# Four full-width RMS norms of a three-block transformer kernel taken apart and folded into the blocks around them

## What is computed

```python
def rmsnorm(x, g):
    xf = x.astype(jnp.float32)
    xf = xf * lax.rsqrt(jnp.mean(xf * xf, axis=-1, keepdims=True) + EPS)
    return xf.astype(x.dtype) * g
...
        u_lat = rmsnorm(h_lat, norms[layer]) * (1 + scale_l[:, None]) + shift_l[:, None]
        u_ctx = rmsnorm(h_ctx, norms[layer]) * (1 + scale_c) + shift_c
...
        hm = _rmsnorm(x, g_mlp)
        x = x + jnp.square(jax.nn.relu(hm @ w_mlp_in)) @ w_mlp_out

    return _rmsnorm(x, g_final)
```

## Time and profile before

| | |
|---|---|
| median of 3 runs | 4933.83 us |
| lowest, highest | 4932.54, 4934.83 us |
| the profiled execution | 4934.28 us |
| span of its profile | 4932.6 us |
| mean granted clock of TensorE | 0.957 |

### The profile page before, as it was taken

How to read it: one execution, slowest core, us unless ns; L and a number is a source line. 1 busy time by engine, 2 the same in 40 slices (tenths; PEclk the granted TensorE clock), 3 DMA queues, 4 the chain that set the end, 5 groups by cost and what they waited for, 6 DMA issues and landing times. The chain is left out here.

```text
span 4932.6 us, 48010 instructions
## 1 busy us (share of the span) xinstructions
PE 4491.0 (91%) x18750; PEld 2645.4 (54%) x18750; DVE 1475.2 (30%) x3439; ACT 941.5 (19%) x1645; POOL 108.7 (2%) x189
## 2 busy tenths in 40 slices
PE   4999998999979999688396999999999979999997
PEld 2676666775537695377142457466454434444443
DVE  2226663662121454344314421111323110000001
ACT  2223332331034111133202421111111010000000
POOL 0000000000000000011001000001000000000000
PEclk8999999999989999799697999999999989999998
DMA  4220003111000111342102110112223111111111
GB/s 182 88 73 8 8 7 71 47 52 69 16 33 29 57 49 52 69 80 43 61 26 73 33 36 30 57 52 77 88 79 115 34 34 39 39 39 39 39 39 43
DMA packets 150801, 258.91 MB, mean 52 GB/s; under 512 B 68545, under 2 KB 91922, under 8 KB 148775
## 3 DMA queue, kind: packets, MB, share of 16 engines
q1 hardware_dynamic: 142664, 240.77, 15.5%
q0 software_dynamic: 7936, 15.35, 1.2%
HBM read 214.82 MB, written 43.53 MB: 52 GB/s over the span
## 5 line engine op out<-in xcount | busy, mean ns | idle before, releaser
L407 PE MATMUL mlp_prod<-sbuf 128*128 128x512 f32 x2048 | 881.2, 593 | 21.3 <-DMA sbuf<-in_w_mlp_in 21.3
L2494 PE MATMUL lat_banks<-sbuf 128*128 128x512 f32 (+2 forms) x2368 | 847.8, 517 | 22.1 <-DMA sbuf<-in_w_in 22.1
L407 PEld LDWEIGHTS mlp_prod<-sbuf 128*128 128x128 f32 x2048 | 389.8, 190 | 512.7 <-issue 490.6
L2494 PEld LDWEIGHTS lat_banks<-sbuf 128*128 128x128 f32 x2368 | 429.1, 206 | 401.3 <-issue 376.9
L1968 PE MATMUL gla_prod<-sbuf 128*128 128x512 f32 (+1 forms) x784 | 324.1, 570 | 27.8 <-DMA sbuf<-in_l_w_in 27.8
L1485 PE MATMUL mls_banks<-sbuf 128*128 128x512 f32 (+1 forms) x768 | 283.9, 524 | 6.8 <-DMA sbuf<-in_l_w_in 6.3
L1968 PEld LDWEIGHTS gla_prod<-sbuf 128*128 128x128 f32 x784 | 149.1, 194 | 183.6 <-issue 150.7
L1485 PEld LDWEIGHTS mls_banks<-sbuf 128*128 128x128 f32 x768 | 144.1, 192 | 123.4 <-issue 109.1
L224 ACT ACTIVATE sbuf<-sbuf 128x1024 f32<-128x1024 f32 (+2 forms) x56 | 56.7, 1024 | 749.6 <-PEq L67 557.1
L2704 ACT ACTIVATE sbuf<-lat_banks 128x512 f32<-128x512 f32 (+1 forms) x124 | 72.3, 583 | 662.0 <-PE lat_banks L2494 610.6
L1030 PE MATMUL mla_banks<-sbuf 128*128 128x512 f32 (+1 forms) x416 | 176.0, 511 | 0.0
(11 more groups left out here) (373 smaller groups left out, 5446.5 us busy)
## 6 DMA issues: line engine op xcount, KB each, us to landing
sbuf<-in_l_w_in SPq DMA_DIRECT2D x59, 512.0 KB, 3.7
sbuf<-in_w_in SPq DMA_DIRECT2D x52, 512.0 KB, 3.7
sbuf<-in_w_mlp_in SPq DMA_DIRECT2D x32, 512.0 KB, 3.5
sbuf<-in_w_mlp_out SPq DMA_DIRECT2D x32, 512.0 KB, 3.4
sbuf<-in_l_w_mod SPq DMA_DIRECT2D x12, 1024.0 KB, 10.2
sbuf<-in_l_w_mod SPq DMA_DIRECT2D x24, 512.0 KB, 4.8
scratch_gates<-sbuf SPq DMA_DIRECT2D x48, 256.0 KB, 2.9
sbuf<-scratch_gates SPq DMA_DIRECT2D x8, 1536.0 KB, 6.7
```

The lines of the kernel that those rows point to most:

```text
L407: last = nc.tensor.matmul(prod[:, n % NB, o:o + 512], w[:, n % NB, k * P:(k + 1) * P], rhs, start=k == 0, stop=k == KD - 1)
L2494: last = nc.tensor.matmul(dst, lhsT, rhs, start=k == 0, stop=k == KD - 1)
```

## The change

Four of the norms ("norm0", "norm1", "mlpnorm", "final2") stop being stages. Each is cut into three parts.

**Sums.** In the block ahead, ACT squares each slab as soon as it is final, and DVE (in `modulation`: POOL) adds the squares up in one tile `total`. Then eight or ten matmuls with one moving column (`column_sums`, L107) turn the tile of sums into `rcol`, one column per 128 tokens.

**Root.** ACT's root and DVE's reciprocal work on those ten (eight, four) columns alone.

**Scaling.** At the head of the next block PE spreads the columns over 128 partitions again, as broadcast weights against the identity (`spread`, L114), DVE scales H into U, and ACT adds the shift, by thirds of the tokens (512, 512, 256; in the MLP by halves). PE's first tile waits for each slab of each third (`normed`). In `mla_block` three memsets of DVE stand ahead of the scaling, and ACT's and DVE's other work of that block behind it.

The load of H moves from the first stage into `modulation`, as eight DMAs on ACT's queue beside the weights on SP's. The g of layer 1 is loaded in `mlstm_block`, g of the MLP and of the last norm in `mlp_block`. In `mlp_block` the last eight down steps become 16 steps of 8 matmuls, first all slabs of one half of the tokens, then all of the other, with their weights held in U; the last norm of the first half runs behind the products of the second, and each finished piece of 128 by 512 is written out by a DMA of its own. Semaphores cleared at the two clearing points are 112 and 128 where they were 100 and 137.

```diff
+def column_sums(nc, bank, acc, ones, tiles):
+    for t in tiles:
+        last = nc.tensor.matmul(bank[:, t:t + 1], acc[:, t * P:(t + 1) * P], ones[:, 0:1], start=True, stop=True)
+    return last
+def spread(nc, bank, rcol, ident, tiles):
+    for a, t in enumerate(tiles):
+        last = nc.tensor.matmul(bank[:, a * P:(a + 1) * P], rcol[:, t:t + 1].broadcast_to([P, P]), ident[:], start=True, stop=True)
+    return last
...
 # modulation
+            for k in range(KD):
+                act.dma_start(H[:, k, :], io["h"][:, k * T:(k + 1) * T]).then_inc(h_in[k], 16)
...
+            for k in range(KD):
+                act.wait_ge(h_in[k], 16)
+                if k >= 3:
+                    act.wait_ge(added, k - 2)
+                nc.scalar.activation(sq[:, k % 2, :] if k else total[:], H[:, k, :], ACT.Square).then_inc(hsq, 1)
+            act.wait_ge(ssum, 1)
+            nc.scalar.activation(rcol[:, 0:TT], stat[:, 0:TT], ACT.Sqrt, bias=eps, scale=1.0 / D).then_inc(rooted, 1)
+        def _(pool):
+            for k in range(1, KD):
+                pool.wait_ge(hsq, k + 1)
+                pool.drain()
+                nc.gpsimd.tensor_tensor(total[:], total[:], sq[:, k % 2, :], ALU.add).then_inc(added, 1)
...
 # mla_block, and with mod1 and GL gla_layer
+                        if t == 0:
+                            pe.wait_ge(normed, KD * (n - first_of[0]) + kk + 1)
...
+            def shift(c):
+                o, wd = thirds()[c]
+                for k in range(KD):
+                    act.wait_ge(lifted, KD * c + k + 1)
+                    for a, n, v in halves_of(o, wd):
+                        last = nc.scalar.activation(U[:, k, a:a + n], U[:, k, a:a + n], ACT.Identity, bias=mod[:, k, v:v + 1])
+                    last.then_inc(normed, 1)
...
+            for c, (o, wd) in enumerate(thirds()):
+                dve.wait_ge(spreaded, c + 1)
+                for kk in range(KD):
+                    for a, n, side in halves_of(o, wd):
+                        last = nc.vector.scalar_tensor_tensor(out=U[:, kk, a:a + n], in0=H[:, kk, a:a + n], scalar=gain[:, kk, side:side + 1],
+                                                              in1=banks[:, 3:6][:, c, a - o:a - o + n], op0=ALU.mult, op1=ALU.mult)
+                    last.then_inc(lifted, 1)
...
 # mlstm_block (latent_block alike, in 16 pieces of 512)
+            for n in range(3 * NO):
+                j, p = divmod(n, 3)
+                o, wd = T3[p]
+                act.wait_ge(oadd, n + 1)
...
+                nc.scalar.activation(osq[:, n % 2, 0:wd] if j else total[:, o:o + wd], H[:, j, o:o + wd], ACT.Square).then_inc(osqd, 1)
...
+                if n >= 4:
+                    add_square(n - 1)
+            add_square(3 * NO - 1)
+            dve.wait_ge(rootc, 1)
+            nc.vector.reciprocal(rcol[:, 0:TT], rcol[:, 0:TT])
...
 # mlp_block, DVE at the end
+            for n, (half, j) in enumerate(ends):
+                dve.wait_ge(end_mm, n + 1)
+                to = acc[:, j, half * 512:half * 512 + 512]
+                nc.vector.tensor_tensor(to, bank(n % 6), to, ALU.add).then_inc(end_add, 1)
+                if n:
+                    add_square(n - 1)
+                if n == 9:
+                    inverse(0)
+                if n >= 11:
+                    finish(0, n - 11)
+            add_square(15)
+            for k in range(5, KD):
+                finish(0, k)
+            inverse(1)
+            for k in range(KD):
+                finish(1, k)
...
 # program
-        load(nc, "start", [(H[:].rearrange("p k t -> p (k t)"), io["h"]), (ones[:], io["ones"]),
-                           (ident[:], io["ident"]), (eps[:], io["eps"])])
+        load(nc, "start", [(ones[:], io["ones"]), (ident[:], io["ident"]), (eps[:], io["eps"])])
...
-        rmsnorm(nc, "mlpnorm", H, KD, D, lat(), U, ones, g_dram=io["g_mlp"], eps_col=eps[:])
-        mlp_block(nc, "mlp", U, NCTX, io["w_mlp_in"], io["w_mlp_out"], H[:, :, NCTX:T])
-        rmsnorm(nc, "final2", H, KD, D, lat(), H, ones, g_dram=io["g_final"], eps_col=eps[:])
-        load(nc, "end", [(io["out"][k * P:(k + 1) * P, :], H[:, k, NCTX:T]) for k in range(KD)])
+        mlp_block(nc, "mlp", U, H, io, rcol, ones, ident, eps[:])
```

More of the change, by code:

```diff
@@ L161, in _ @@
             turn(NC - 1)
+            pe.wait_ge(added, KD - 1)
+            column_sums(nc, stat, total, ones, range(TT)).then_inc(ssum, 1)
         @block.vector
@@ L409, in _, with end_step, sums_of, spread_out @@
                 last.then_inc(mm_done, 1)
+            def end_step(n):
+                half, j = ends[n]
+                if half == 0:
+                    pe.wait_ge(end_ready[j], 16)
+                if n < 6:
+                    pe.wait_ge(added, downs[NS] - 3 + n // 2)
+                else:
+                    pe.wait_ge(end_add, n - 5)
+                for k in range(KD):
+                    if n == 0:
+                        pe.wait_ge(squared, 3 * KD + k + 1)
+                    last = nc.tensor.matmul(bank(n % 6), x[:, j, k * P:(k + 1) * P], hid[:, 1, k, half * 512:half * 512 + 512],
+                                            start=k == 0, stop=k == KD - 1)
+                last.then_inc(end_mm, 1)
+            def sums_of(half):
+                pe.wait_ge(sq_add, (KD - 1) * (half + 1))
+                if half == 0:
+                    pe.wait_ge(added, downs[NS])
+                for a in range(4):
+                    last = nc.tensor.matmul(bank(7)[:, a:a + 1], total[:, (4 * half + a) * P:(4 * half + a + 1) * P], ones[:, 0:1],
+                                            start=True, stop=True)
+                last.then_inc(ssum, 1)
+            def spread_out(half):
+                pe.wait_ge(rinvd, half + 1)
+                spread(nc, bank(6 + half), rcol, ident, range(4 * half, 4 * half + 4)).then_inc(spreaded, 1)
+            for n in range(10):
+                end_step(n)
+            sums_of(0)
+            end_step(10)
+            spread_out(0)
+            for n in range(11, 16):
+                end_step(n)
+            sums_of(1)
+            spread_out(1)
         @block.scalar
@@ L1562, in _ @@
                 last.then_inc(omm, 1)
+            for p, (o, wd) in enumerate(T3):
+                pe.wait_ge(added, 3 * (NO - 2) + p + 1)
+                last = column_sums(nc, banks[:, 2], total, ones, range(o // P, (o + wd) // P))
+            last.then_inc(ssum, 1)
         @block.scalar
@@ L1790, in _ @@
             dve.drain()
-            dve.wait_ge(const_in, 48)
+            dve.wait_ge(const_in, 64)
+            for v in range(2):
+                nc.vector.scalar_tensor_tensor(out=gain[:, :, v], in0=mod1[:, KD:2 * KD, v], scalar=1.0, in1=g1[:], op0=ALU.add, op1=ALU.mult)
             exponents(0)
@@ L2657, in _ @@
                 last.then_inc(oprod, 1)
+            for half in range(2):
+                pe.wait_ge(added, 13 + half)
+                last = column_sums(nc, banks[:, 2], total, ones, range(4 * half, 4 * half + 4))
+            last.then_inc(ssum, 1)
         @block.scalar
```

233 lines of the change are left out of this document (178 added, 55 removed).

## The result

| | before | changed |
|---|---|---|
| median us | 4933.18 (4 runs, 4928.94 to 4934.83) | 4768.77 (4 runs, 4766.76 to 4769.26) |
| profiled execution: time, span | 4934.28, 4932.6 | 4769.26, 4767.6 |
| mean granted clock | 0.957 | 0.967 |

The two spans differ by 165.0.

A forecast was written before the change was run, and what follows sets the result against it. The prediction took PE's row of products as the bound, with wins only where PE has none. Joint savings 41.1 + 44.9 + 31.2 + 30.8 = 148.0, taken off the median 4933.83, gave 4786 us, range 4777 to 4803.

The forecast's parts named there:

- What bounds the kernel: PE's products, busy 4491.0 of 4932.6 us; with their number unchanged, time can be won only where PE has none.
- The four joints: Gaps from a block's last useful matmul to the next's first, or the span's end; 207.7 us in all, 148.0 saved.
- joint 1: Start to layer 0: first product at 64.6 us instead of 105.75, saving 41.1.
- joint 2: mLSTM to layer 1 (gla): length 14.9 us instead of 59.8, saving 44.9.
- At the end: Joint 4, last product to span's end: 15.4 us instead of 48.2; 30.8 saved after 2.0 for PE's inner sums and spreads.
- Costed at nothing: Squares and adds behind output products, and POOL's seven adds in modulation, were taken as hidden, adding no time.
- POOL late: Rival in modulation: adds of 8.15 us end 15 us after PE is ready; 4801 us, chance 0.07.
- starving heads: Rival in joints 1 and 2: slabs scaled and shifted serially, 2.05 us each, cost 19 us; 4805, chance 0.08.
- longer stage changes: Rival: larger blocks lengthen each stage change, 5 to 15 us in all; 4791 to 4801 us, chance 0.04.
- a clock that stays down: Rival: PE stays at 1.2 GHz in four places, losing 158 us; 4944 us, chance 0.03.
- a saving lost in stalls: Rival: the saving returns as stalls inside the blocks; no change, 4934 us, chance 0.01.
- The restarts get faster: Rival: much shorter gaps remove the 2.8 us lost to the lower clock at each restart; 4777 us, chance 0.09.

The follow-up runs named there:

- the pair of held kernels: Changed kernel with 18 DVE memsets ahead of gla's scaling, without or with nine PE matmuls just before gla's first product: 4797.24 and 4796.01 us.
- The first held kernel: Changed kernel with 18 DVE memsets ahead of gla's scaling, PE left idle between its spread and first product: 4797.24 us.
- the kernel with joint 1 alone: Kernel before with only the start, modulation and layer 0 part of the change: 4880.68 us.
- the two repeats: Both kernels run again unchanged: 4932.01 us before and 4767.13 changed; later 4930.39 and 4932.05 before, 4772.52 changed.
- the fillings tried here: Changed kernel with unread matmuls in PE's waits: at two heads 4764.27 us; at more places 4769.15 with 30 per mix wait, 4766.21 with 47.

## Why the prediction was off

**What bounds the kernel** was right for the joints: there the win came where PE had nothing useful to do, and the engines' shares said nothing about it. It was wrong as the general rule that it was written as, that a change which leaves the number of products alone "can only win at places where PE has none": 12.1 us came from untouched stages, 8.1 of them while PE was at work.

**The four joints** were right, to 0.7 us each in the first pair of profiles, and by the means of four to 1.4 (joint 1, 42.5 instead of 41.1, where the stage varies by over 2 us from execution to execution) and 0.7 (the others). Small terms missed in both directions. The spread ran at half clock in all joints (4.40 to 4.61 us for ten). In joint 2 DVE started 2.09 us behind its start, forecast 0.9 to 1.8; with 0.2 us more in the chain ahead of it and 0.2 more for the first shift this made 15.58 of 14.9. At the end four spreads took 2.08, forecast 1.0. In joint 1 two misses met: the last product began at 50.07 instead of 51.0, but then its 16 records took 3.33 us at a clock that was partly half, where the forecast had taken the 1.92 of before. The last scalings took 0.67 us each in a row, not 0.72 to 0.75, and gave this back. The clearing of semaphores (SP's next DMA 7.4 us after the reciprocal) and the first weights' way were as forecast.

**Costed at nothing.** POOL's adds took 2.88 to 2.92 us each and ended at 47.14, 8 us before PE was ready for them; the estimate from the Trainium skill (GPSIMD Engine Reference, section 3.1), 2.8 us, fits, and the low bound from DVE's rows, 1.6, did not. The squares and adds behind the products are hidden: the MLP lasts 1.6 us more, which the inner sums and spreads (1.7) account for, and PE is busy in every us of the first 18.95 of layer 0 and the first 19.60 of gla.

**The rivals.** POOL late, starving heads, longer stage changes (SP's next DMA 7.4 us behind the reciprocal, as forecast), a clock that stays down (1.00 in the MLP from 3872.00 on) and a saving lost in stalls did not occur. *The restarts get faster* did, at two of three heads (layer 0 and gla; the granted clock went from 0.91 and 0.87 to 1.00), for another reason than the one given. I had put it down to the gap's length; the pair of held kernels shows for gla that PE's work right ahead of the first product does it. It is not sure to: in one of the four executions layer 0's clock stayed at half for 6.1 us behind the first product, although the spread had ended 1.5 us ahead of it as in the others (0.84 over the first 18.95 us). And the MLP's head did not gain (0.88 over its first 17 us before, 0.89 now), although eight spreads of 3.76 us end 0.82 us ahead of it. In the kernel with 30 matmuls in the mix stage, whose MLP is the same, that head did start at full clock (1.00 over 17 us). What decides between the two is not shown.

**The step that failed** is the premise above, by which what lies between the joints was put at nothing without a reason, and with it the sum, "41.1 + 44.9 + 31.2 + 30.8 = 148.0", taken off the median as if every stage between the joints kept its length, and so the range, whose lower end allowed 9 us there and gave it a chance of 0.09. On the mean of four profiles those stages gave 12.1. Of these the heads account for 2.1 (gla's first 80 records) and, in three of four executions, 1.8 (layer 0: its first 288 records last 117.7 instead of 119.5 us; in the fourth 120.8), 3.2 on the mean. The larger part of the rest, some 5 us by the estimate above, is fewer or shorter stretches at half clock inside the stages, most of them worth 1.7 each: behind waits such as 3.8 us in the latent block and 7.1 in gla, but also where PE had only short idle times, in layer 0's attention (three stretches in each execution of before, one or two in the changed kernel) and at one place of the latent block (behind waits of 0.7 and 1.0 us). In the kernel before, both places of the latent block slow down in each of four executions; in the changed kernel one of the two does. The last 4 us are not the clock and stay open.

The Trainium skill (TensorE: Matmul & The Clock Gate, part 1) says that throttled is the default state and that activity releases it; by the rows above (0.50 without a record of PE ahead of the spread, 1.00 from gla's first product on), the trace agrees. The same part says that the loss at a restart varies from run to run. Here it does in some stages (memory norm, 93.3 to 97.6), while gla's first 80 records took 33.62 to 33.73 in four executions of before.

**What stays open** is why the changed kernel loses such stretches in layer 0's attention and in the latent block. It does not hang on the new code of these blocks. The first held kernel, in which against the changed one joint 2 alone is altered, kept 394.9 us and three stretches in layer 0's attention, as before, where the changed kernel has 391.5 to 393.2; and the kernel with joint 1 alone has the old latent code and loses one of the two stretches there. And the time that a comparison of medians gives, 164.4 here, 164.2 and 158.2 in the two repeats, scatters about the 161.1 of the profiles' mean by some 3 us either way.

## What to carry to other kernels

A chain between two blocks can be forecast link by link, to under 1 us, from rows of other places in the same profile. What lies between the touched places isn't free of the change when TensorE's clock moves with its idle times: look at the granted clock of every restart, count the stretches at half clock inside long blocks (here most were worth 1.7 us) and let the range hold a few of them both ways, also where PE only has short idle times between its products, and take several profiles of the same kernel before explaining 5 us by one. A head is more likely to start at full clock if PE has worked up to 1 or 2 us ahead of it: over all profiles with the new heads, gla did in eight of eight (at the latest 1.8 us behind its first product), layer 0 in six of ten, the MLP in one of ten. None of the fillings tried here beat the changed kernel by more than its runs vary (4764.27 and 4766.21 against 4767.13 to 4771.44), though a mix stage got 5.5 us shorter.

## What was not expected of the hardware

- Filler ahead of a wait is worth nothing if it ends early: with 4.85 us idle behind it two matmuls of 512 columns took 3.78 us, with 1.06 us 1.98; over 2.00 us of idleness gla still started at full clock.
- Stages of over 500 us repeat to 0.4 us in four executions of the kernel before (1245.2 to 1245.6, 585.3 to 585.5, 1014.0 to 1014.3, 880.5 to 880.7), and change by 2 to 4 us in another kernel with the same products in them, where two of them also vary more (1239.8 to 1243.0, 581.5 to 582.9).
- The clock can fall without a long wait: in layer 0's attention (450.50 to 454.00, 0.51) it did where no idle time of PE ahead of it was above 0.7 us.
- The start stage varies most (105.2 to 110.4 us in seven executions with the old start, 63.3 to 68.6 in ten with the new one): up to 1.7 us of that are the last 16 records of the modulation, which took 1.92 to 3.64 us, by the clock; the rest was not taken apart.
